# Stick-breaking layer: the running sums in rounded products, two passes of queues, lanes in at rounds 0, 3 and 8

## The reference

```python
z = einsum('bhqd,bhkd->bhqk', q, k) * SB_SCALE            # 0.125
log_beta = log_sigmoid(z)
log_keep = where(strict, log_sigmoid(-z), 0)              # strict: key before query
between = cumsum(log_keep, reverse=True) - log_keep       # over later keys
a = where(strict, exp(log_beta + between), 0)
o = a @ v
```

## Time and profile before

| what | us |
|---|---|
| median of the runs | 2209.06 |
| profiled execution | 2210.41 |
| its span | 2209.1 |
| TensorE busy | 2049.4 (93%) |
| weight loads busy | 1622.4 (73%) |
| VectorE busy | 1126.6 (51%) |
| ScalarE busy | 872.0 (39%) |
| POOL busy | 27.2 (1%) |
| DMA | 169.64 MB, mean 77 GB/s |

### The profile page before, as it was taken

How to read it: one execution, slowest core, us unless ns; L and a number is a source line. 1 busy time by engine, 2 the same in 40 slices (tenths; PEclk the granted TensorE clock), 3 DMA queues, 4 the chain that set the end, 5 groups by cost and what they waited for, 6 DMA issues and landing times.

```text
span 2209.1 us, 28369 instructions
## 1 busy us (share of the span) xinstructions
PE 2049.4 (93%) x11400; PEld 1622.4 (73%) x11400; DVE 1126.6 (51%) x2014; ACT 872.0 (39%) x1567; POOL 27.2 (1%) x68
## 2 busy tenths in 40 slices
PE   6888888899988999999999999999989999999997
PEld 5765666677756578978888887677567978888886
DVE  5666468737466455445343345344455445443344
ACT  5325443245343444434232233465644344232232
POOL 0000000000000000000000000011100000000000
PEclk9989899999989799999999999999999999999999
DMA  5210011012211023212222222111123312222321
GB/s 197 86 48 21 20 48 58 3 59 99 86 41 56 1 96 115 96 62 95 101 96 96 101 92 95 58 58 48 39 77 105 108 64 96 96 100 91 105 94 69
DMA packets 52051, 169.64 MB, mean 77 GB/s; under 512 B 5776, under 2 KB 9424, under 8 KB 51920
## 3 DMA queue, kind: packets, MB, share of 16 engines
q1 hardware_dynamic: 51920, 167.82, 21.7%
HBM read 165.70 MB, written 2.10 MB: 76 GB/s over the span
## 4 chain that ended last, share of the span: by engine, by line
PE 63%; DVE 3%; ACT 2%; issue 1%; POOL 0%; DVEq 0%; ACTq 0%
PE ps L152 62%; PE ps L157 1%; DVE X L1523 0%; DVE st L403 0%; DVE macc L233 0%; ACT sa_sp L2103 0%; DVE x_pr L390 0%; ACT sb_sp L2103 0%; ACT msq L226 0%; ACT sa_sp L2106 0%; ACT sa_sp L2101 0%; ACT sb_sp L2106 0%; ACT sb_sp L2101 0%; DVE lo L1431 0%; DVE st L1615 0%
## 5 line engine op out<-in xcount | busy, mean ns | idle before, releaser
L152 PE MATMUL ps<-hi,wr 128*128 128x512 f32 (+1 forms) x4616 | 1407.7, 385 | 50.7 <-DVE wr L171 34.3
L152 PEld LDWEIGHTS ps<-hi,wr 128*128 128x128 f32 x4616 | 862.4, 190 | 230.7 <-DVE wr L171 25.7
L152 PE MATMUL ps<-lo,wr 128*128 128x512 f32 (+1 forms) x2308 | 880.4, 381 | 0.0
L152 PEld LDWEIGHTS ps<-lo,wr 128*128 128x128 f32 x2308 | 440.0, 191 | 84.5 <-issue 3.9
L165 ACT ACTIVATE wr<-raw 128x1024 fp32r<-128x1024 f32 x293 | 307.7, 1052 | 349.3 <-PE ps L152 349.3
L171 DVE TENSOR_TENSOR wr<-raw,wr 128x1024 fp32r<-128x1024 f32 x293 | 356.7, 1217 | 4.3 <-ACT wr L165 2.3
L1450 DVE TENSOR_TENSOR X<-X,ps 128x512 f32<-128x512 f32 x96 | 66.0, 687 | 238.1 <-PE ps L152 238.1
L1986 ACT ACTIVATE mlp<-mlp 128x512 f32<-128x512 f32 x64 | 40.4, 632 | 207.8 <-DVE mlp L1969 207.8
L1969 DVE SCALAR_TENSOR_TENSOR mlp<-ps,R 128x512 f32<-128x512 f32 x64 | 44.2, 691 | 113.2 <-PE ps L152 106.2
L213 ACT ACTIVATE hi<-X,pv 128x512 fp32r<-128x512 f32 x48 | 34.7, 722 | 138.4 <-DVE X L1450 135.9
L1972 DVE TENSOR_TENSOR lo<-mlp,hi 128x512 fp32r<-128x512 f32 x64 | 44.3, 692 | 87.8 <-ACT hi L1990 87.8
(11 more groups left out here) (694 smaller groups left out, 1912.6 us busy)
## 6 DMA issues: line engine op xcount, KB each, us to landing
raw<-d_w SPq DMA_DIRECT2D x128, 512.0 KB, 3.4
raw<-d_wkv SPq DMA_DIRECT2D x32, 512.0 KB, 3.4
raw<-d_w_in SPq DMA_DIRECT2D x30, 512.0 KB, 3.5
raw<-d_sb_w_in SPq DMA_DIRECT2D x24, 512.0 KB, 3.4
raw<-d_ev_w_in SPq DMA_DIRECT2D x16, 512.0 KB, 3.5
raw<-d_wq SPq DMA_DIRECT2D x16, 512.0 KB, 3.4
raw<-d_wo SPq DMA_DIRECT2D x16, 512.0 KB, 3.5
X<-d_xT SPq DMA_DIRECT2D x16, 256.0 KB, 5.1
```

The source lines that it names most:

```text
L152: return pe.matmul(out, lhsT, rhs, start=start, stop=stop, skip_group_check=True)
```

## The change

- The softplus is kept as two rounded numbers (`hi`, and `lo` for the rest), and the sums are products of type `float32r` with rounded copies of `ntri` and `nones` (made once, in place, by ScalarE). Instead of a running sum, the products with `nones` run over every later block i > j.
- VectorE makes `hi`, then the rest (max(score, 0) - hi), then `lo` = rest + ln part: three steps a head and stage instead of one, in tiles of their own; `hi` of j = 0 lies over q and k.
- The mask is added to the scores before the softplus, so a masked score's softplus is zero. POOL does nothing any more.
- The factor 0.125 is folded into the evacuation of q. Y is copied by ScalarE.
- Each engine's work on a pair is split in two generators. `sb_layer` weaves all lanes' main parts first and behind them, in the same round, all lanes' second parts: the sums on TensorE, hi, rest and lo on VectorE, the weights and Y on ScalarE. The lanes begin at rounds 0, 3 and 8.

```diff
+    if scale is not None:
+        v.scalar_tensor_tensor(out=dst, in0=K.bank(*key)[0:m, 0:dst.shape[1]], scalar=scale, in1=R, op0=ALU.mult,
+                               op1=ALU.mult).then_inc(*K.tell("dve", *key, frees=key))
+        return
...
-        for hh in range(2):
-            b, sp, old = K.bank(*k, "s", j, hh), L.sp[hh][j % 2], L.sp[hh][1 - j % 2]
-            pe.wait_ge(*K.done("pool", *k, "sp", j, hh))
-            done = mm(pe, b[:, 0:n], M.C("ntri"), sp[:, 0:n], False, j == 3)
-            if j < 3:
-                if j < 2:
-                    pe.wait_ge(*K.done("dve", *k, "run", j + 1, hh))
-                done = mm(pe, b[:, 128:n], M.C("nones"), old[:, 0:n - 128], False, True)
-            done.then_inc(*K.tell("pe", *k, "c", j, hh))
...
+def sb_sums_tensor(K, M, pe, z, L):
+
+    k = ("sb", z)
+    for _ in range(3):
+        yield
+    for j in (3, 2, 1, 0):
+        n = T - j * 128
+        yield
+        for hh in range(2):
+            b = K.bank(*k, "s", j, hh)
+            pe.wait_ge(*K.done("act", "tri"))
+            pe.wait_ge(*K.done("dve", *k, "lo", j, hh))
+            for i in range(3, j, -1):
+                at = (i - j) * 128
+                mm(pe, b[:, at:n], M.nones, sb_parts(L.hi, hh, i), False, False)
+                mm(pe, b[:, at:n], M.nones, sb_parts(L.lo, hh, i), False, False)
+            mm(pe, b[:, 0:n], M.ntri, sb_parts(L.hi, hh, j), False, False)
+            mm(pe, b[:, 0:n], M.ntri, sb_parts(L.lo, hh, j), False, True).then_inc(*K.tell("pe", *k, "c", j, hh))
...
+    evac(K, M, v, (*k, "q"), L.q, M.R, scale=0.125)
...
+            v.tensor_tensor(b[:, 0:128], b[:, 0:128], M.C("sbm"), ALU.add).then_inc(*K.tell("dve", *k, "mask", j, hh))
...
+            v.scalar_tensor_tensor(out=sb_parts(L.hi, hh, j), in0=K.bank(*k, "s", j, hh)[:, 0:n], scalar=0.0,
+                                   in1=sb_parts(L.w, hh, j), op0=ALU.max, op1=ALU.add).then_inc(
+                *K.tell("dve", *k, "hi", j, hh))
         for hh in range(2):
-            b, sp, old = K.bank(*k, "s", j, hh), L.sp[hh][j % 2], L.sp[hh][1 - j % 2]
-            v.wait_ge(*K.done("pe", *k, "c", j, hh))
-            v.tensor_tensor(b[:, 0:128], b[:, 0:128], M.C("sbm"), ALU.add).then_inc(*K.tell("dve", *k, "diag", j, hh))
-            if 0 < j < 3:
-                v.tensor_tensor(sp[:, 128:n], sp[:, 128:n], old[:, 0:n - 128], ALU.add).then_inc(
-                    *K.tell("dve", *k, "run", j, hh))
-        yield
-    v.wait_ge(*K.done("pe", *k, "o"))
-    v.tensor_copy(M.Y[z], K.bank(*k, "o")).then_inc(*K.tell("dve", "Y", 4, z, frees=(*k, "o")))
+            v.wait_ge(*K.done("dve", *k, "hi", j, hh))
+            v.scalar_tensor_tensor(out=sb_parts(L.rest, hh, j), in0=K.bank(*k, "s", j, hh)[:, 0:n], scalar=0.0,
+                                   in1=sb_parts(L.hi, hh, j).bitcast(F32), op0=ALU.max, op1=ALU.subtract).then_inc(
+                *K.tell("dve", *k, "rest", j, hh))
+        for hh in range(2):
+            v.wait_ge(*K.done("dve", *k, "rest", j, hh))
+            v.tensor_tensor(sb_parts(L.lo, hh, j), sb_parts(L.rest, hh, j), sb_parts(L.w, hh, j),
+                            ALU.add).then_inc(*K.tell("dve", *k, "lo", j, hh))
...
+        a.activation(M.tri, M.cst[:, COFF["ntri"][0]:COFF["ntri"][0] + 256], ACT.Copy).then_inc(*K.tell("act", "tri"))
...
+            a.wait_ge(*K.done("dve", *k, "mask", j, hh))
+            a.activation(sp, K.bank(*k, "s", j, hh)[:, 0:n], ACT.Abs).then_inc(*K.tell("act", *k, "abs", j, hh))
...
+            a.wait_ge(*K.done("pe", *k, "c", j, hh))
+            a.activation(sb_parts(L.w, hh, j), K.bank(*k, "s", j, hh)[:, 0:n], ACT.Exp).then_inc(
...
+    a.wait_ge(*K.done("pe", *k, "o"))
+    a.activation(M.Y[z], K.bank(*k, "o"), ACT.Copy).then_inc(*K.tell("act", "Y", 4, z, frees=(*k, "o")))
...
-def sb_layer(M, sb):
+def sb_layer(M, main, behind):
+
     A, B, C = M.sb.lanes
-    weave(chain(sb(0, A), sb(3, A), sb(6, A)), chain(idle(4), sb(1, B), sb(4, B), sb(7, B)),
-          chain(idle(8), sb(2, C), sb(5, C)))
+    weave(*(chain(idle(n), *(part(z, L) for z in pairs)) for part in (main, behind)
+            for n, L, pairs in ((0, A, (0, 3, 6)), (3, B, (1, 4, 7)), (8, C, (2, 5)))))
...
```

More of the change, by code:

```diff
@@ L1995, with sb_parts @@
 OD = ("n", 4)
-def sb_parts(L, hh, j):
-    tile, o = {3: (L.w[hh], 384), 1: (L.w[hh], 0), 2: (L.w[2], hh * 256), 0: (L.w[3 + hh], 0)}[j]
+def sb_parts(tiles, hh, j):
+    tile, o = {3: (tiles[hh], 384), 1: (tiles[hh], 0), 2: (tiles[2], hh * 256), 0: (tiles[3 + hh], 0)}[j]
     return tile[:, o:o + T - j * 128]
@@ L2022, in sb_tensor @@
             if j == 3 and hh == 0:
-                pe.wait_ge(*K.done("dve", *k, "q8"))
                 pe.wait_ge(*K.done("dve", *k, "k"))
@@ L2062, in sb_vector, with sb_softplus_vector @@
     for j in (3, 2, 1, 0):
+        for hh in range(2):
+            b = K.bank(*k, "s", j, hh)
+            v.wait_ge(*K.done("pe", *k, "s", j, hh))
+            v.tensor_tensor(b[:, 0:128], b[:, 0:128], M.C("sbm"), ALU.add).then_inc(*K.tell("dve", *k, "mask", j, hh))
+        yield
+        yield
+    yield
+def sb_softplus_vector(K, M, v, z, L):
+    k = ("sb", z)
+    for _ in range(3):
+        yield
+    for j in (3, 2, 1, 0):
         n = T - j * 128
         for hh in range(2):
[L2065 removed]
             v.wait_ge(*K.done("act", *k, "ln", j, hh))
[L2067 to L2076 removed]
+            v.scalar_tensor_tensor(out=sb_parts(L.hi, hh, j), in0=K.bank(*k, "s", j, hh)[:, 0:n], scalar=0.0,
+                                   in1=sb_parts(L.w, hh, j), op0=ALU.max, op1=ALU.add).then_inc(
+                *K.tell("dve", *k, "hi", j, hh))
+        for hh in range(2):
+            v.wait_ge(*K.done("dve", *k, "hi", j, hh))
+            v.scalar_tensor_tensor(out=sb_parts(L.rest, hh, j), in0=K.bank(*k, "s", j, hh)[:, 0:n], scalar=0.0,
+                                   in1=sb_parts(L.hi, hh, j).bitcast(F32), op0=ALU.max, op1=ALU.subtract).then_inc(
+                *K.tell("dve", *k, "rest", j, hh))
+        for hh in range(2):
+            v.wait_ge(*K.done("dve", *k, "rest", j, hh))
+            v.tensor_tensor(sb_parts(L.lo, hh, j), sb_parts(L.rest, hh, j), sb_parts(L.w, hh, j),
+                            ALU.add).then_inc(*K.tell("dve", *k, "lo", j, hh))
+        yield
         yield
[L2078 to L2079 removed]
     yield
@@ L2096, in sb_scalar @@
         for hh in range(2):
[L2097 to L2101, removed]
+            sp = sb_parts(L.w, hh, j)
+            a.wait_ge(*K.done("dve", *k, "mask", j, hh))
+            a.activation(sp, K.bank(*k, "s", j, hh)[:, 0:n], ACT.Abs).then_inc(*K.tell("act", *k, "abs", j, hh))
             a.wait_ge(*K.own("act"))
-            a.activation(sp[:, 0:n], sp[:, 0:n], ACT.Exp, scale=-1.0).then_inc(*K.tell("act", *k, "en", j, hh))
+            a.activation(sp, sp, ACT.Exp, scale=-1.0).then_inc(*K.tell("act", *k, "en", j, hh))
             log_table(K, a)
             a.wait_ge(*K.own("act"))
-            a.activation(sp[:, 0:n], sp[:, 0:n], ACT.Ln, bias=M.PV("one")).then_inc(*K.tell("act", *k, "ln", j, hh))
-        yield
[L2108 to L2126, removed]
+            a.activation(sp, sp, ACT.Ln, bias=M.PV("one")).then_inc(*K.tell("act", *k, "ln", j, hh))
         yield
@@ L2129, in sb_pool, with sb_weights_scalar @@
     yield
-def sb_layer(M, sb):
+def sb_weights_scalar(K, M, a, z, L):
+    k = ("sb", z)
+    for _ in range(3):
+        yield
+    for j in (3, 2, 1, 0):
+        n = T - j * 128
+        yield
+        for hh in range(2):
+            a.wait_ge(*K.done("pe", *k, "c", j, hh))
+            a.activation(sb_parts(L.w, hh, j), K.bank(*k, "s", j, hh)[:, 0:n], ACT.Exp).then_inc(
+                *K.tell("act", *k, "aw", j, hh, frees=(*k, "s", j, hh)))
+        yield
+    a.wait_ge(*K.done("pe", *k, "o"))
+    a.activation(M.Y[z], K.bank(*k, "o"), ACT.Copy).then_inc(*K.tell("act", "Y", 4, z, frees=(*k, "o")))
+    yield
+def sb_layer(M, main, behind):
     A, B, C = M.sb.lanes
-    weave(chain(sb(0, A), sb(3, A), sb(6, A)), chain(idle(4), sb(1, B), sb(4, B), sb(7, B)),
-          chain(idle(8), sb(2, C), sb(5, C)))
+    weave(*(chain(idle(n), *(part(z, L) for z in pairs)) for part in (main, behind)
+            for n, L, pairs in ((0, A, (0, 3, 6)), (3, B, (1, 4, 7)), (8, C, (2, 5)))))
 def tensor_program(K, M, pe):
@@ L2316, in build @@
         M.R, M.acc, M.sq = tile("R", 16), tile("acc", 17), tiles("sq", 18, 2)
-        M.by_dve = [(0, i) for i in range(8)] + [(1, i) for i in range(4)] + [(4, i) for i in range(8)]
+        M.by_dve = [(0, i) for i in range(8)] + [(1, i) for i in range(4)]
         g = M.first = Memory()
@@ L2406, in build @@
         s.lanes = Memory(), Memory(), Memory()
[L2407 to L2410, removed]
+        for L, name, at_ in zip(s.lanes, ("sa_", "sb_", "sc_"), (
+                [*range(20, 32), 44, 45, 18, 19], [*range(32, 44), *(plain(0, i) for i in range(12, 16))],
+                [*(plain(0, i) for i in range(12)), 17, 13, 14, 15])):
```

(9 more changed lines are left out.)

19 lines of the change are left out of this document (8 added, 11 removed).

## The result

The changed kernel takes 2224.9 us (median; 2215.6 to 2229.9) against 2205.4 us of the kernel before beside it (2201.1 to 2211.0): the ratio is 1.0081 [1.0056, 1.0106]. So the sign of the prediction was right and the size was not: +18 us by the ratio, where +9 was forecast. The median lies inside the range for 8 in 10 (2203 to 2232) and 2 us above the forecast's own (2213 to 2223). The profiled execution took 2226.0 us, of which the span is 2224.7.

A forecast was written before the change was run, and what follows sets the result against it. TensorE was taken to bound the steady part, and the stage chain's latency wherever no dense product covers it. 2210.4 - 10.9 (sums) + 18.8 (stalls) + 1 (clock) = 2219.3 us profiled, 2218 median; own range 2213 to 2223, 8 in 10 2203 to 2232.

The forecast's parts named there:

- the sign of the prediction: Whole kernel: slower, 2219.3 us profiled and 2218 as a median; slower was given 0.65.
- Stalls: TensorE's waits in the odd layer: the longer softplus chain, bare in rounds without dense products, adds 18.8 us.
- pair 0's waits at the start: Pair 0, j = 3: lane B's round 3 product covers them, so stalls of 1.9 and 0.45 us go, -2.8.
- the walk: Stall-by-stall count of TensorE's idle through the odd layer's rounds with estimated step durations: +18.8 us as a whole.
- The saving on the sums: Sums on TensorE: rounded products save 1.35 us a pair, 10.9 us over eight pairs.
- The narrow product at 0.112: Sums on TensorE: price in us assumed for one rounded product of 128 columns.
- the range taken: Price of a 128-column rounded product: 0.067 (5.8 us more saved) to 0.225 (14.5 us less).
- rivals 1 and 3: Narrow products: 1, 0.225 like plain ones, 2228 us, chance 0.2; 3, 0.067 to 0.08, 2213 to 2215, chance 0.12.
- The clock: Odd layer: lower-clock stretches fewer at the start, with more places later, mostly swallowed by waits; +1 us.
- Rival 2: Steady part covers the chain, C's sums (j = 0) wait under 1 us: faster, 2204.7 us profiled; chance 0.18.
- Rival 4: Steady part: three or more stretches at the lower clock, +5, 2223 us; chance 0.08.
- the 60% given: VectorE in the layer: rest and lo add 42 us, yet its share stays under 60%, costing nothing.

The follow-up runs named there:

- e1: Changed kernel with lane B entering at round 4 instead of 3: 2215.0 us against 2209.2 of the kernel before, ratio 1.0033.
- e3: Changed kernel (lanes 0, 3, 8) with VectorE doing hi, rest, lo of one head before the next: 2217.4 us, ratio 1.0040 to the kernel before.
- e6: Changed kernel without rest and lo, the products taking hi twice: 2203.5 us against 2206.2 of the kernel before, ratio 0.9987.
- e7: Changed kernel with each lane's second part right behind its own main part: 2246.2 us against 2206.2 of the kernel before, ratio 1.0182.
- e4: Changed kernel with lane B at round 4 and VectorE's steps head by head: 2205.4 us against 2209.2 of the kernel before, ratio 0.9985.
- e5: Changed kernel with 84 idle products ahead of seven groups of sums: 2218.0 us against 2206.2 of the kernel before, ratio 1.0054.
- e8: Changed kernel, lane B at round 4, VectorE head by head, 16, 15 and 18 idle products in three tail waits: 2193.4 us, ratio 0.9954 to the kernel before.
- e11: Repeat: changed kernel, lane B at round 4, VectorE head by head, 16, 15 and 18 idle tail products: 2199.7 us, ratio 0.9961 to the kernel before.
- e10: Control: changed kernel, lane B at round 4, VectorE head by head, one idle product in each of three tail waits: 2203.4 us, ratio 0.9983.
- e2: Kernel before with only lane B entering at round 3 instead of 4: 2215.5 us against 2209.2, ratio 1.0033.

## Why the prediction was right in sign and half in size

- **Stalls: as walked, a little smaller.** C's sums at j = 0 waited 3.47 and 3.40 us (3.3 forecast), pair 6's 5.00 and pair 7's 6.94 (5 to 7 forecast for each), all released by lo; pair 0's waits at the start are gone. In sum idle rose by 14.7 us where the walk had 18.8. The walk counted a drain of 0.17 with each stall, which stands in the busy time here; with six more stalls (18 against 12) that is 1 us of the difference. e1, e3, e6 and e7 each moved these waits as the mechanism asks.
- **The saving on the sums: 8.4 us instead of 10.9.** Both heads take 2.55 us at j = 0 (2.5 forecast), and 1.7, 1.0 and 0.5 at j = 1, 2, 3: 5.75 a pair against 6.8, so 1.05 saved and not 1.35. A small part of the miss is arithmetic: 6.82 less the prediction's own 5.53 is 1.29 a pair, so 10.3 us and not 10.9. The narrow product at 0.112 was near enough: a pair of narrow ones takes 0.17, which is 0.085 for one, but a 256 behind it gives 0.05 back. This agrees with neither end of the range taken, and rivals 1 and 3 fall. The Trainium skill's 81 ns for a narrow pair of load and matmul (TensorE: Matmul & The Clock Gate, Back-to-back issue gap) is near that 0.085. The 4 us more that would be saved by it did not come, for the reason just named.
- **The clock: the step that failed.** It was put at +1 us with ends of -5 and +5, in the words "most of them among waits that swallow it". From the prices of the products busy time should have been 244.4 - 8.4 = 236.0 us; it is 246.2, so 10.2 us came where 1 stood. The mean of 0.92 over 278.4 us means some 44 us at 1.2 GHz (278.4 x 0.08 x 2), against 10 before (261.8 x 0.02 x 2). They lie around rounds 7, 18 and 30 and in much of the tail. Counted in another way: TensorE is busy in 34.0 of the 44.3 us, which it would have done in half of that at the full clock, so 17 us are lost, against 5 before: 12 more. By either count it is 10 to 12 us, not 1; about 1 of the first count is the drains named above. The waits swallow only the part in which TensorE is idle (10.3 us). The products behind a wait are themselves a link of what comes next, since the weights wait for the sums and the next softplus for the scores, and they run at half speed (2.48 against 1.28 us above).
- **The sum.** Layer forecast 261.8 - 10.9 + 18.8 + 1 = 270.7; measured 278.4. The difference of 7.7 is 2.5 (saving) - 4.1 (idle) + 9.2 (clock), with 0.1 of rounding. That the first two nearly cancel is luck: had the waits come as walked, the forecast would have been off by 4 us more.
- **The rivals.** Rival 2 (faster) fell at its own mark: C's sums wait 3.4 us, not under 1. Rival 4 named the true mechanism but looked for it in the steady part, where the clock is 0.98 and 1.00 but for rounds 18 and 19 (0.79), and priced it at 5 us. No dense product waited for weights, and VectorE's 141.5 of 278.4 us stayed under the 60% given.

Shown are: the waits and their releaser, the effect of the lanes and of the order on VectorE (e1, e3, e4), and that idle products shorten the layer at a higher clock (e5; e8 and e11 against e10). Open is what the lanes 0, 3, 8 add to the busy time besides the clock (some 4.5 of the 8.5 us in e2, the 5.1 us between e3 and e4), and the exact share of the clock in the medians: e5's profiled layer gained 10 us, its median about 6. The part ahead of the layer, which none of the edits touches, runs from 1347.8 to 1360.5 us between single executions, so a total of one profile can't settle it.

## What to carry to other kernels

Price a stall twice: the wait itself, and the products behind it at the lower clock, most of all where these products are themselves the chain that the next wait hangs on. When a chain over two engines grows, put the first consumer's steps first in each in-order queue, and look at the rounds where no dense product covers it before looking at totals. If such waits can't be removed, products that nobody reads, placed ahead of them, are worth a measured try.

## What the runs showed of the hardware that was not expected

- The granted clock fell to the lower level (1.2 GHz) inside a wait: of the wait of 3.47 us (1481.71 to 1485.18) the stretch from 1482.0 to 1483.2 has a mean of 1.00 and that from 1483.4 to 1484.0 one of 0.50. Ahead of it stood a wait of 1.31 us and 1.15 us of work (1480.56 to 1481.71). Where idle products stood in the waits the layer's clock was 0.99 to 1.00.
- For the cost of such stretches the Trainium skill takes half of the time at the low clock (TensorE: Matmul & The Clock Gate, HAM oscillation — how this bites in real kernels). By that the 44 us would be an estimated 22 us. Here e5, with 3.4 us at the low clock left, puts it at 12, since TensorE is idle in 10 of the 44 us; the measurement decides.
- Lanes that enter at 0, 3, 8 instead of 0, 4, 8 raised busy time for the same products by 8 us in two pairs of kernels (e2 against before, the changed kernel against e1). It is not the clock alone: e3 and e4 have the same 0.96 and are still 5.1 us apart. What the rest is no run here shows.
